# Moving the transposes of a head's keys from the next head's first slot to the head's own last slot

## The reference

```
f = lb + (1 - lb) * sigmoid(fz);  k = (1 - lb) * sigmoid(-fz)
S_t = diag(f_t) S_{t-1} + k_t v_t^T ;   o_t = S_t^T q_t      # per head, per token
o = o * rsqrt(mean(o^2) + eps) * norm_g * sigmoid(g)
```

## Time and profile before

| | |
|---|---|
| median of 3 runs | 1202.02 us (1201.29 to 1203.36) |
| the profiled execution | 1200.96 us |
| its span, first to last instruction | 1199.2 us |
| TensorE busy | 98% of the span, 9718 matmuls |
| VectorE, ScalarE, GpSimd busy | 68%, 42%, 15% |
| mean granted TensorE clock | 0.997 |

### The profile page before, as it was taken

How to read it: one execution, slowest core, us unless ns; L and a number is a source line. 1 busy time by engine, 2 the same in 40 slices (tenths; PEclk the granted TensorE clock), 3 DMA queues, 4 the chain that set the end, 5 groups by cost and what they waited for, 6 DMA issues and landing times.

```text
span 1199.2 us, 24092 instructions
## 1 busy us (share of the span) xinstructions
PE 1169.8 (98%) x9718; PEld 1129.0 (94%) x9718; DVE 814.6 (68%) x1498; ACT 507.8 (42%) x850; POOL 181.1 (15%) x152
## 2 busy tenths in 40 slices
PE   9999999999898999999999999999999999999996
PEld 8988889998788999999999999999999999999995
DVE  6995767557887557798627863686458844786547
ACT  5411212337756446665314541354125521554335
POOL 5210000100000244200210021001200030001365
PEclk9999999999999999999999999999999999999999
DMA  8441223518435410411372227222631255112503
GB/s 301 117 119 50 89 78 122 179 58 220 123 105 183 178 36 37 142 37 46 89 258 90 55 64 273 98 65 55 227 146 55 56 181 191 55 56 60 206 25 119
DMA packets 84815, 139.31 MB, mean 116 GB/s; under 512 B 26360, under 2 KB 52504, under 8 KB 84696
## 3 DMA queue, kind: packets, MB, share of 16 engines
q1 hardware_dynamic: 84704, 137.77, 35.9%
HBM read 97.89 MB, written 40.03 MB: 115 GB/s over the span
## 4 chain that ended last, share of the span: by engine, by line
PE 84%; DVE 10%; ACT 2%; issue 2%; DMA 1%; POOL 0%; SPq 0%; POOLq 0%; ACTq 0%; DVEq 0%
PE psum L1973 32%; PE psum L1945 15%; PE psum L1657 13%; PE psum L1676 6%; PE psum L2056 5%; PE psum L1734 4%; PE psum L1646 1%; DMA st<-in_xT 1%; DVE R L2583 1%; PE psum L1787 1%; PE psum L1769 1%; DVE wl L2631 1%; PE psum L1782 1%; PE psum L1854 1%; PE psum L1816 1%
## 5 line engine op out<-in xcount | busy, mean ns | idle before, releaser
L1973 PE MATMUL psum<-XH,wh 128*128 128x258 f32 x640 | 181.3, 283 | 1.7 <-ACT ub L1324 1.4
L1973 PE MATMUL psum<-XH,wl 128*128 128x258 f32 x640 | 181.0, 283 | 0.0
L1973 PE MATMUL psum<-TR,wh 128*128 128x258 f32 x640 | 181.0, 283 | 0.0
L1973 PE MATMUL psum<-XL,wh 128*128 128x258 f32 x640 | 180.0, 282 | 0.0
L1587 POOL TENSOR_TENSOR wl<-raw,wh 128x512 fp32r<-128x512 f32 (+2 forms) x36 | 57.8, 1610 | 567.8 <-ACT wh L1273 557.1
L1945 PE MATMUL psum<-AH,wl 128*128 128x344 f32 x384 | 123.1, 321 | 0.0
L1973 PEld LDWEIGHTS psum<-XH,wh 128*128 128x128 f32 x640 | 121.0, 189 | 2.2 <-issue 2.2
L1945 PE MATMUL psum<-AL,wh 128*128 128x344 f32 x384 | 123.1, 320 | 0.0
L1945 PE MATMUL psum<-AH,wh 128*128 128x344 f32 x384 | 122.9, 320 | 0.0
L1973 PEld LDWEIGHTS psum<-XL,wh 128*128 128x128 f32 x640 | 121.5, 190 | 0.1
L1973 PEld LDWEIGHTS psum<-XH,wl 128*128 128x128 f32 x640 | 120.9, 189 | 0.0
(11 more groups left out here) (413 smaller groups left out, 2807.5 us busy)
## 6 DMA issues: line engine op xcount, KB each, us to landing
raw<-in_w_up SPq DMA_DIRECT2D x44, 512.0 KB, 4.1
ub<-rscr SPq DMA_DIRECT2D x16, 516.0 KB, 5.0
rscr<-ub SPq DMA_DIRECT2D x16, 516.0 KB, 3.2
raw<-in_w_dn SPq DMA_DIRECT2D x32, 256.0 KB, 3.3
raw<-in_w_units SPq DMA_DIRECT2D x15, 512.0 KB, 4.5
fscr<-st SPq DMA_DIRECT2D x10, 516.0 KB, 2.9
R<-in_xT SPq DMA_DIRECT2D x8, 516.0 KB, 6.7
RS<-rscr SPq DMA_DIRECT2D x8, 516.0 KB, 4.4
```

The costliest lines, as they stand in the source:

```text
L1973: ins = nc.tensor.matmul(psum[:, bank, 0:QW], a[:, k * P:(k + 1) * P], x, start=(start and p_ == 0), stop=(stop and p_ == 2), skip_group_c ...
```

## The change

In SLOTS the step `kt` leaves the string of level 0 of heads 1, 2 and 3. A new step `kt+`, which means the transposes of the same head, stands at the end of the string of level 7 of heads 0, 1 and 2. In rows 0 and 1 the two parts of the level-7 slot are split around `b+`. The transposes of head 3 stay in TAIL. The number of parts between one level and the next level is unchanged.

```diff
--- before.py
+++ after.py
@@ -108,10 +108,10 @@
     ("v 1", "1", "1", "2", "3", "8", "1", ""),
 ]
 SLOTS = [
-    ("1 1", "2", "2", "2 load+ 1", "2 s0", "sig+ 2 vb", "2 a+ 1", "2 b+"),
-    ("2 kt", "1 kv 1", "1 o save 1", "1 ms0 1 load+ ms1", "1 s0 ms2 1", "1 vb sig+ f0 1", "1 f1 a+ 1 y", "f2 2 b+"),
-    ("1 kt x gelu0", "1 kv 1 gelu1", "1 o save gl0", "ms0 1 ms1 gelu2 load+ gl1 gelu3", "1 s0 gl2 ms2 q3 gl3", "1 sig+ f0 f1 f2 glu 2", "2 a+ vb 1", "1 b+"),
-    ("1 kt 1", "1 kv 1 mld0", "2 o save", "1 ms0 1 ms1 f0", "1 s0 1 ms2 mld1 f1 f2", "2 z out 2 zh 1 zl mld2 wload", "1 mix0 1 mix1", "1 ml0 vb ml1 mix2 1 ml2"),
+    ("1 1", "2", "2", "2 load+ 1", "2 s0", "sig+ 2 vb", "2 a+ 1", "1 b+ 1 kt+"),
+    ("2", "1 kv 1", "1 o save 1", "1 ms0 1 load+ ms1", "1 s0 ms2 1", "1 vb sig+ f0 1", "1 f1 a+ 1 y", "f2 1 b+ 1 kt+"),
+    ("1 x gelu0", "1 kv 1 gelu1", "1 o save gl0", "ms0 1 ms1 gelu2 load+ gl1 gelu3", "1 s0 gl2 ms2 q3 gl3", "1 sig+ f0 f1 f2 glu 2", "2 a+ vb 1", "1 b+ kt+"),
+    ("2", "1 kv 1 mld0", "2 o save", "1 ms0 1 ms1 f0", "1 s0 1 ms2 mld1 f1 f2", "2 z out 2 zh 1 zl mld2 wload", "1 mix0 1 mix1", "1 ml0 vb ml1 mix2 1 ml2"),
 ]
 TAIL = "kt 1 kv 2 o save rload wh2 wl2 2 ms0 1 ms1 1 f30 m30 ms2 1 f31 l30 m31 f32 ahead p30 l31 m32 wh3 l32 p31 p32"
 
@@ -158,6 +158,8 @@
             o.append(("s0_scale", h))
         elif step == "vb":
             o.append(("vb", h))
+        elif step == "kt+":
+            o.append(("kt", h))
         elif step in ("kt", "kv", "o"):
             o.append((step, h - 1))
         elif step in ("f0", "f1", "f2"):
```

## The result

The changed kernel takes 1203.75 us (median of 16 runs, 1202.97 to 1207.37) against 1202.49 us before (16 runs, 1201.06 to 1204.18). The ratio is 1.0016, with a 95% interval of 1.0008 to 1.0023: 1.9 us slower, between 1.0 and 2.8. That is real, and inside what the prediction called no change (2.4 us). The two medians lie only 1.26 us apart; the changed kernel's runs reach further up, and the means (1204.33 and 1202.50) lie 1.8 us apart.

The account below looks back on a forecast made before the run. TensorE, busy 98% of the span, was taken as the bound, so only its idle time near the moves counts: 0.43 - 0.54 + 1.29 = +1.18 us on the 1202.02 median gives 1203.2 us, range 1200.8 to 1205.4.

Parts of the forecast that it names:

- Place 1: Head 0 to 1: first scores wait for ScalarE's copy of the transposed keys, behind a weight split; second scores +0.43 us.
- Place 2: Head 1 to 2: ScalarE's copy waits for VectorE's previous head output, yet second scores come sooner, at 294.23; -0.54 us.
- Place 3: Head 2 to 3: transposes wait for VectorE, first scores for ScalarE's copy behind sigmoid and weight split; +1.29 us.
- about 1 us of new idle time: Head 2 to 3: TensorE free at about 330.83, transposes start at 331.82 after VectorE's last pass over the keys.
- ScalarE's part: Head 2 to 3: sigmoid and weight split precede the key copy; first scores wait some 1.5 us for it.
- The sum: The three places, heads 0 to 3, together: 0.43 - 0.54 + 1.29 = +1.18 us, giving 1203.2 us.
- rival A: Head 2 to 3: the granted clock falls in the new idle time, 1.7 us more, 1204.9 us; chance 0.13.
- Rival B: Line 1816: the 3.2 us hole, a late fetch, goes with its slow clock; -4.9 us, 1198.3 us; chance 0.06.
- Rival C: At the moved transposes only the old waits count and go: -2.4 us, 1199.6 us; chance 0.06.
- Rival D: All three places: waits are exchanged and sum to zero; low end of the forecast, no separate chance.
- No transfer or queue is passed, the slip stays to the end: SP's and POOL's queues unchanged; TensorE has matmuls without gaps from 406 us, so the slip remains; no size.
- ScalarE's early S5 copies gain nothing: Head 1 to 2: S5 output copies come some 2 us sooner, but their VectorE split stands behind a later step.

Follow-up runs that it names:

- place 2 alone: Only the move at head 1 to 2, the other two undone, against the kernel before: 1202.18 us against 1201.90, ratio 0.9999.
- second profile of the changed kernel: The changed kernel unaltered, profiled once more: 1206.32 us.
- first profile: The changed kernel with all three moves, profiled for the result; its runs have ratio 1.0016 to the kernel before, median 1203.75 us.
- place 3 alone: Only the move at head 2 to 3, the other two undone, against the kernel before: 1203.77 us, ratio 1.0011.

## Why the prediction was right, point by point

- **Place 1, +0.43.** Measured +0.40 (9.51 against 9.11), and the same in every profile with this order. The step by which it comes (copy behind the weight split, first scores behind the copy) is in the timeline line by line. Shown.
- **Place 2, -0.54.** Measured -0.52 (7.96 against 8.48) in the first pair of profiles, and 7.77 or 7.96 against 8.30 to 8.48 over all. Shown. The two values differ by what ends last: with 7.96 ScalarE's copy waits for VectorE's line 2445, as predicted, and with 7.77 (place 2 alone, second profile of the changed kernel) line 2445 is done sooner and the copy, at 292.02 in place 2 alone, waits for the transposes themselves.
- **Place 3, +1.29.** The mechanism was right and the size was off in two ways that work against each other. At full clock it cost +0.48: the "about 1 us of new idle time" before the transposes was 0.16 us in the first profile and 0.44, 0.58 and 0.94 in three others, since VectorE is late by less when the hole has held TensorE up (in the first profile TensorE reached the last level 1.23 us later than with place 3 alone, VectorE its last pass over the keys 0.68 us later, 331.44 against 330.76). ScalarE's part, 1.5 us of waiting, was as predicted. But in three of four profiles the granted clock fell there, and the intervals were 11.19, 11.33 and 12.81. The mean of the four is 11.1 against 8.5 of the three other profiles with the old order at place 3 (8.71, 8.50, 8.43) and the same order on ScalarE and of the transfers; with places 1 and 2 that makes about +2.5 us, as an estimate from few profiles, where 1.9 (1.0 to 2.8) was measured.
- **The sum, +1.18.** It lies inside the measured interval, nearer to its low end. That it does is in part luck: the idle time before the transposes was put 0.8 us above that of the first profile, and the clock's fall, left out of the forecast, cost more than that in three of four. It is one that no single execution showed: 0.4 at full clock, or 2 and more with the clock's fall. The mis-sized steps are these: place 3 at full clock, +1.29 for +0.48, and rival A's chance, 0.13, for three of four profiles; the prediction reasoned from the old holes of up to 1.2 us, which had left the clock alone, and gave too little to the fact that the new idle time comes in two pieces with only transposes between.
- **Rival B** (the fetch hole goes by the change itself) did not happen: 3.2 to 3.6 us in all profiles with the old transfers. That its cause is a fetch behind data is supported, not proved, by the held-back transfer, after which the packet came sooner and the hole halved, and by the steady 2.2 to 2.6 us from packet to next matmul. **Rival C** (the waits just go) is out: 2.4 us went and 2.8 came. **Rival D** was near the truth at full clock.
- **No transfer or queue is passed, the slip stays to the end:** true; the last stage takes 800.8 to 800.9 us in each profile. It does so although TensorE's matmuls are not without gaps from 406 us on, as the prediction says: six waits stand there, 4.7 us in all, the same before and after. That ScalarE's early S5 copies gain nothing was not measured by itself.

Left open: why the clock stayed up at place 3 in one of four executions. It is the one with the least idle time there (0.16 and 1.50 us, against 0.44, 0.58 or 0.94 and 1.49), but idle time alone does not decide, as the two waits for the state sums show, which are equal in all profiles and brought the clock down in one.

## What to carry to other kernels

When a step moves on the engine that is the bound, follow its result through the in-order queue of the engine that empties it: here 1.65 us of sigmoid and weight split stood ahead of a 0.6 us copy, and reordering that one queue took the loss away as far as it can be measured. Look at the idle time between two dense stretches together, since waits of 0.44 and 1.49 us with light work between them brought the clock down where a single hole of 1.63 us had not; it is a risk and no certainty, as one execution of four kept its clock. And where a stretch has two bounds, one a transfer and one another engine's work, removing either alone showed nothing (1202.07 against 1201.80 us, and 1200.97 against 1201.07); the pair gave 2.2 us (1201.07 to 1198.83).

## What the runs showed of the hardware that was not expected

- TensorE stood 3.2 to 3.6 us in the middle of 64 equal matmuls in every profile with the old transfers, while one packet of 16 KB on the instruction queue was served among data traffic at full share. Holding one 512 KB broadcast back by 3.9 us, with three transfers sooner by it, brought that packet forward and the hole to 1.63 us (2.19 in another kernel). The Trainium skill ("Runtime: NRT & Kernel Launch", instruction fetch mechanics) says that such fetches run ahead and are mostly hidden. If this hole is a fetch, as the 2.2 to 2.6 us from packet to next matmul in all 14 profiles suggest, here one was not.
- The granted clock fell after idle time of 3.2 us and of 2.19 us in one piece, stayed up after 1.63 us, and fell also where TensorE had been idle for 0.44 us and 1.49 us with eight transposes between. A fall cost 1.7 us or 3.4 us of clock, no value between, in all 14 profiles. The same order in the same kernel can lose nothing (first profile, place 3), 1.7 or 3.4.
